# A depthwise convolution's taps on TensorE: from full diagonals, one tap at a time, to stacked diagonals in four column tiles, four taps at a time

## The reference, cut to what matters

```python
def conv_mixer(h, w_pw1, b_pw1, w_dw, b_dw, cg, cb, w_out, b_out):
    a, gt = jnp.split(h @ w_pw1 + b_pw1, 2, axis=-1)
    y = a * jax.nn.sigmoid(gt)
    y = lax.conv_general_dilated(y, w_dw[:, None, :], window_strides=(1,), padding='SAME',
                                 dimension_numbers=('NWC', 'WIO', 'NWC'),
                                 feature_group_count=D_MODEL) + b_dw
    y = jax.nn.silu(layer_norm(y, cg, cb))
    return y @ w_out + b_out
```

## Time and profile before

| What | us |
|---|---|
| Time before, median of 3 runs | 3671.02 |
| Lowest and highest of them | 3669.53, 3674.19 |
| Span of the profiled execution | 3670.5 |
| TensorE busy in it | 3537.7 (96%) |
| VectorE busy | 2182.4 (59%) |
| ScalarE busy | 1522.9 (41%) |
| GpSimd busy | 389.3 (11%) |

### The profile page before, as it was taken

One profiled execution on the slowest core, in us unless ns is written; L12 is line 12 of the kernel. 1 busy time (PEld: TensorE's weight loads), 2 busy tenths in 40 slices (PEclk: granted clock), 3 DMA queues, 4 the chain that ended last, 5 costly groups with the idle time before them and its releaser, 6 DMA issues. The chain is left out here.

```text
span 3670.5 us, 45735 instructions
## 1 busy us (share of the span) xinstructions
PE 3537.7 (96%) x18060; PEld 2922.5 (80%) x18060; DVE 2182.4 (59%) x2931; ACT 1522.9 (41%) x1713; POOL 389.3 (11%) x315
## 2 busy tenths in 40 slices
PE   8999999999999999999998999999998998999998
PEld 6888888756888888888758888877887777888886
DVE  7545446538654467556897433553226236999998
ACT  4111111537422233222446222453545235778776
POOL 2000000200120011000111100100000002333331
PEclk9999999999999999999999999999999998999999
DMA  6323323210244335444202322231221325999997
GB/s 258 125 81 104 115 89 102 66 58 1 70 149 138 111 119 171 144 156 160 72 21 70 103 92 98 81 117 55 86 69 62 117 101 204 365 366 360 366 374 297
DMA packets 315246, 522.43 MB, mean 142 GB/s; under 512 B 18517, under 2 KB 274562, under 8 KB 289217
## 3 DMA queue, kind: packets, MB, share of 16 engines
q1 hardware_dynamic: 304032, 507.06, 39.8%
q0 software_dynamic: 11040, 12.91, 1.0%
HBM read 519.91 MB, written 25.17 MB: 149 GB/s over the span
## 5 line engine op out<-in xcount | busy, mean ns | idle before, releaser
L541 PE MATMUL banks<-operand_hi,trunk_weights_hi 128*128 128x512 f32 (+1 forms) x1568 | 566.9, 362 | 21.5 <-DVE operand_lo L939 5.7
L541 PE MATMUL banks<-operand_lo,trunk_weights_hi 128*128 128x512 f32 (+1 forms) x1568 | 556.8, 355 | 0.0
L541 PE MATMUL banks<-operand_hi,trunk_weights_lo 128*128 128x512 f32 (+1 forms) x1568 | 556.7, 355 | 0.0
L541 PEld LDWEIGHTS banks<-operand_hi,trunk_weights_hi 128*128 128x128 f32 x1568 | 297.2, 190 | 69.3 <-issue 14.4
L541 PEld LDWEIGHTS banks<-operand_hi,trunk_weights_lo 128*128 128x128 f32 x1568 | 297.2, 190 | 41.9
L541 PEld LDWEIGHTS banks<-operand_lo,trunk_weights_hi 128*128 128x128 f32 x1568 | 297.4, 190 | 41.4 <-issue 0.5
L4311 DVE TENSOR_TENSOR ex_w_lo<-weight_ring,ex_w_hi 128x2048 fp32r<-128x2048 f32 x128 | 291.7, 2293 | 41.7 <-ACT ex_w_hi L4239 41.7
L1335 DVE TENSOR_TENSOR trunk_weights_lo<-weight_ring,trunk_weights_hi 128x2048 fp32r<-128x2048 f32 x90 | 206.1, 2290 | 176.9 <-ACT trunk_weights_hi L1290 176.9
L4239 ACT ACTIVATE ex_w_hi<-weight_ring 128x2048 fp32r<-128x2048 f32 x128 | 245.2, 1917 | 76.9 <-PE banks L4137 63.9
L1290 ACT ACTIVATE trunk_weights_hi<-weight_ring 128x2048 fp32r<-128x2048 f32 x90 | 171.7, 1908 | 216.5 <-PE banks L541 216.4
L541 PE MATMUL banks<-trunk_hidden_hi,trunk_weights_hi 128*128 128x512 f32 (+1 forms) x672 | 233.2, 347 | 3.4 <-DVE trunk_hidden_lo L1353 1.4
(11 more groups left out here) (612 smaller groups left out, 7451.6 us busy)
## 6 DMA issues: line engine op xcount, KB each, us to landing
weight_ring<-ffn_w SPq DMA_DIRECT2D x120, 1024.0 KB, 5.2
weight_ring<-w_mod SPq DMA_DIRECT2D x72, 1024.0 KB, 5.1
weight_ring<-w_gate SPq DMA_DIRECT2D x64, 1024.0 KB, 6.8
weight_ring<-w_up SPq DMA_DIRECT2D x64, 1024.0 KB
room<-w_down SPq DMA_DIRECT2D x64, 1024.0 KB, 7.2
weight_ring<-w_in SPq DMA_DIRECT2D x26, 1024.0 KB, 5.2
weight_ring<-ffn_w SPq DMA_DIRECT2D x16, 768.0 KB, 4.3
weight_ring<-o_w_pw SPq DMA_DIRECT2D x8, 1024.0 KB, 5.3
```

The lines of the kernel that those rows point to most:

```text
L541: ins = pe.matmul(bank[:, at:at + width], w, x[:, at:at + width], start=start and n == 0, stop=stop and n == len(passes) - 1)
```

## The change

TensorE's share of the taps is now done in fours. For a block b of 32 channels of a tile, four copies of Y's 32 rows, shifted by 0, 1, 2 and 3 tokens, are stacked on the 128 partitions. One product with a 128x32 stationary operand, four 32x32 diagonals one under the other, then does four taps of 32 channels. Four such products, one a block, write to PSUM partitions 0, 32, 64 and 96 and so use four column tiles of TensorE. A group g is these four products; it does taps 4g to 4g+3 of a tile.

- `GROUPS_ON_PE` is 4 for tiles 0 to 5 (16 taps, before 10 or 11) and 7 for tiles 6 and 7 (28 taps, before 12). VectorE has 15 taps left a tile, and 3 for the last two.
- The stacked copies are made by DMAs that ScalarE issues, 16 a tile (`act_shifts`), into three sets of buffers. They lie in unused room: the spare, the third region of the split weights, and `acc`.
- GpSimd makes the stacked diagonals from a folded identity, 16 or 28 small instructions a tile (`pool_taps`), from columns that VectorE has spread over the partitions in 16 copies (`dve_columns`). The diagonals lie in the second half of `k.X`.
- TensorE waits once a tile for the diagonals and the copies, and signals once.
- At the end, ScalarE's first weight split of the next stage waits for tile 5's taps, and VectorE adds tiles 4 and 5 after its own taps of the last pair.

```diff
         if m >= 4:
             pe.wait_ge(self.s_out, m - 3)
-        for w in range(ON_PE[m]):
-            n = self.first_diag[m] + w
-            pe.wait_ge(self.s_diag, n + 1)
-            pe.matmul(self.bank(m), self.diag[:, n % 8, :], self.Y[:, m, w:w + S], start=w == 0, stop=w == ON_PE[m] - 1).then_inc(self.s_tap, 1)
-
-    def act_diagonals(self, act, upto):
-        for n in range(self.n_diag, upto):
-            m = max(j for j in range(KD) if self.first_diag[j] <= n)
-            if n >= 8:
-                act.wait_ge(self.s_tap, n - 7)
-            act.activation(self.diag[:, n % 8, :], self.k.ident[:], ACT.Copy, scale=self.wdw((n - self.first_diag[m]) * KD + m)).then_inc(self.s_diag, 1)
-        self.n_diag = upto
+        pe.wait_ge(self.s_diag, m + 1)
+        pe.wait_ge(self.s_shift[m % 3], (m // 3 + 1) * 16 * STACK * STACK)
+        for g in range(GROUPS_ON_PE[m]):
+            for b in range(STACK):
+                ins = pe.matmul(self.bank(m)[b * BLOCK:(b + 1) * BLOCK], self.tap(m, b, g), self.shifted[m % 3][b][:, STACK * g:STACK * g + S],
+                                start=g == 0, stop=g == GROUPS_ON_PE[m] - 1)
+        ins.then_inc(self.s_tap, 1)
+
+    def tap(self, m, b, g):
+        n = b * MAX_GROUPS + g
+        return self.taps[:, 4 * (m % 2) + n // 8, BLOCK * (n % 8):BLOCK * (n % 8) + BLOCK]
+
+    def act_shifts(self, act, m):
+        if m == 0:
+            act.wait_ge(self.s_edges, 2)
+        act.wait_ge(self.s_value, m + 1)
+        if m >= 3:
+            act.wait_ge(self.s_tap, m - 2)
+        width = S + STACK * (GROUPS_ON_PE[m] - 1)
+        for b in range(STACK):
+            for j in range(STACK):
+                act.dma_start(self.shifted[m % 3][b][j * BLOCK:(j + 1) * BLOCK, 0:width],
+                              self.Y[b * BLOCK:(b + 1) * BLOCK, m, j:j + width]).then_inc(self.s_shift[m % 3], 16)
+
+    def dve_columns(self, dve):
+        first = COLUMN["o_w_dw"]
+        of_taps = self.k.col[:, first:first + STACK * MAX_GROUPS * KD].rearrange("p (g j m) -> p j m g", j=STACK, m=KD)
+        for b in range(STACK):
+            for j in range(STACK):
+                dve.tensor_copy(self.columns[j * BLOCK:(j + 1) * BLOCK, :, b, :], of_taps[b * BLOCK:(b + 1) * BLOCK, j, :, :]).then_inc(self.s_spread, 1)
+
+    def pool_taps(self, pool, m):
+        if m == 0:
+            pool.wait_ge(self.s_spread, STACK * STACK)
+        if m >= 2:
+            pool.wait_ge(self.s_tap, m - 1)
+        for b in range(STACK):
+            for g in range(GROUPS_ON_PE[m]):
+                ins = pool.tensor_scalar(self.tap(m, b, g), self.k.fold[:], self.columns[:, m, b, g:g + 1], 0.0, ALU.mult, ALU.add)
+        ins.then_inc(self.s_diag, 1)
...
         self.act_hi(act, 0, 3, 0)
+        for m in (0, 1):
+            self.act_shifts(act, m)
         for q in range(1, 4):
             if q < 3:
                 self.act_hi(act, 0, 2 * q + 2, 0)
             self.act_gates(act, 2 * q)
-            self.act_diagonals(act, min(upto(2 * q - 2) + 8, upto(2 * q)))
             if q < 3:
                 self.act_hi(act, 0, 2 * q + 3, 0)
-            self.act_diagonals(act, upto(2 * q))
+            for m in (2 * q, 2 * q + 1):
+                self.act_shifts(act, m)
...
-        for step in range(TAPS - min(ON_PE[m] for m in pair)):
+        for step in range(TAPS - STACK * GROUPS_ON_PE[2 * q]):
...
-ON_PE = (10, 10, 11, 11, 11, 11, 12, 12)
+STACK = P // BLOCK
+GROUPS_ON_PE = (4, 4, 4, 4, 4, 4, 7, 7)
+MAX_GROUPS = 7
+SHIFTED = S + STACK * (MAX_GROUPS - 1)
...
             for kk in range(KD):
                 n10.pool_rescale(pool, kk)
+                if kk == 3:
+                    conv.pool_taps(pool, 0)
+                    conv.pool_taps(pool, 1)
+            for m in range(2, KD):
+                conv.pool_taps(pool, m)
...
             conv.act_rest(act, lambda kk: n10.act_keep(act, kk))
+            act.wait_ge(conv.s_tap, 6)
             back.act_chunk(act, 0)
```

More of the change, by code:

```diff
@@ L360, in load_and_modulate @@
             sem("vectors_copied"), sem("silu"), sem("cond_hi"), sem("cond_lo"))
-        s_hi, s_lo, s_done, s_xt, s_xa, s_xd, s_row, s_gate, s_cols, s_ch, s_pad = (
+        s_hi, s_lo, s_done, s_xt, s_xa, s_xd, s_row, s_gate, s_cols, s_ch, s_pad, s_fold = (
             sem("w_hi"), sem("w_lo"), sem("products"), sem("x_turned"), sem("x_copied_act"), sem("x_copied_dve"), sem("mod_rows"),
-            sem("gate_rows"), sem("mod_columns"), sem("chain"), sem("cond_padded"))
+            sem("gate_rows"), sem("mod_columns"), sem("chain"), sem("cond_padded"), sem("fold"))
         block = st.enter_context(nc.Block())
@@ L402, in _ @@
             k.n_vec = n
+            pool.wait_ge(s_con, 16)
+            for i in range(0, P, BLOCK):
+                pool.tensor_copy(k.fold[i:i + BLOCK, :], k.ident[i:i + BLOCK, i:i + BLOCK]).then_inc(s_fold, 1)
         @block.tensor
@@ L1506, with __init__ @@
 class Convolution(Opening):
-    def __init__(self, k, st, name, bufs, base, Y, out, tmp, diag):
-        self.k, self.base, self.Y, self.out, self.tmp, self.diag = k, base, Y, out, tmp, diag
+    def __init__(self, k, st, name, bufs, base, Y, out, tmp, shifted, taps, columns):
+        self.k, self.base, self.Y, self.out, self.tmp = k, base, Y, out, tmp
+        self.shifted, self.taps, self.columns = shifted, taps, columns
         self.h_hi, self.h_lo, self.w_hi, self.w_lo = bufs
@@ L1516, in __init__ @@
             sem("weights_hi"), sem("weights_lo"), sem("tiles"), sem("gates"), sem("values"), sem("edges"))
-        self.s_diag, self.s_tap, self.s_acc, self.s_out = sem("diagonals"), sem("taps"), sem("sums"), sem("convolved")
+        self.s_spread, self.s_diag, self.s_tap, self.s_acc, self.s_out = (
+            sem("tap_columns"), sem("diagonals"), sem("taps"), sem("sums"), sem("convolved"))
+        self.s_shift = [sem(f"shifted{i}") for i in range(3)]
         self.loads = 8
@@ L1520, in __init__ @@
         self.n_acc = 0
-        self.first_diag = [sum(ON_PE[:m]) for m in range(KD + 1)]
-        self.n_diag = 0
     def sync(self, sp):
@@ L1624, in dve_taps @@
         last = {}
-        for step in range(TAPS - min(ON_PE[m] for m in pair)):
+        for step in range(TAPS - STACK * GROUPS_ON_PE[2 * q]):
             for m in pair:
-                w = ON_PE[m] + step
-                if w >= TAPS:
-                    continue
+                w = STACK * GROUPS_ON_PE[m] + step
                 x, out = self.Y[:, m, w:w + S], self.out[:, m, 0:S]
@@ L1657, in dve_rest @@
             self.dve_taps(dve, q, during)
+            if q == 3:
+                self.dve_out(dve, (4, 5))
             if q < 2:
@@ L1686, in region @@
         if c == 3:
-            return self.spare[part][:]
+            return self.spare[part]
         at = SLOT * (2, 0, 1)[c]
@@ L2040, in trunk @@
             conv_out = convolved.enter_context(nc.sbuf_tensor("trunk_convolved", [P, KD, S], F32))
-            spare = [convolved.enter_context(nc.sbuf_tensor(f"trunk_spare{i}", [P, SLOT], F32R)) for i in range(2)]
+            both = convolved.enter_context(nc.sbuf_tensor("trunk_spare", [P, 2 * SLOT], F32R))
+            spare = [both[:, SLOT * i:SLOT * i + SLOT] for i in range(2)]
+        pieces = lambda x, n, at=0: [x[:, at + SHIFTED * i:at + SHIFTED * i + SHIFTED].bitcast(F32) for i in range(n)]
+        in_spare, in_hi, in_lo = pieces(both, 7), pieces(w_hi, 3, 2 * SLOT), pieces(w_lo, 1, 2 * SLOT)
+        acc_row = acc[:].rearrange("p a b -> p (a b)")
+        n_columns = KD * STACK * MAX_GROUPS
+        shifted = [in_spare[0:4], in_spare[4:7] + [acc_row[:, n_columns:n_columns + SHIFTED]], in_hi + in_lo]
+        columns = acc_row[:, 0:n_columns].rearrange("p (m b g) -> p m b g", m=KD, b=STACK)
         bufs = (h_hi, h_lo, f_hi, f_lo, w_hi, w_lo, tmp, acc)
@@ L2047, in trunk @@
         conv = base(Convolution(k, st, "c_in", in_bufs, at[-1], room[:].rearrange("p (k t) -> p k t", k=KD), conv_out, tmp,
-                                acc[:].rearrange("p a (b c) -> p (a b) c", c=P)))
+                                shifted, k.X[:, :, S:S + HALF], columns))
         back = base(Halves(k, st, "c_out", in_bufs, spare, at[-1]))
```

8 lines of the change are left out of this document (5 added, 3 removed).

## The result

The changed kernel takes 3677.09 us (median of 20 runs, 3668.77 to 3685.65), the one before 3669.78 us beside it (20 runs). The ratio is 1.0019, with a 95% interval of 1.0013 to 1.0026: 7 us slower, by less than the 0.2% named in the prediction. The forecast was 3655, and 3671 the end of its range.

The account below looks back on a forecast made before the run. TensorE and VectorE were taken as balanced bounds of the stage. The walk's 24 us gain less 3 for the clock and 5 for GpSimd slowing VectorE gave 16 us less, so 3655 us; range 3640 to 3671 (0.82).

Parts of the forecast that it names:

- TensorE's part: TensorE's taps: 38 groups of four overlapping products at 0.87 us a group, 32.8 us in place of 76.0.
- Rivals 1 and 2: TensorE's taps: 1, half overlap, 1.73 us a group, 3664, chance 0.13; 2, no overlap, 3727 or 3757, chance 0.09.
- VectorE's part: VectorE's taps: loses 64 of 160, 42.6 us; gains 16 copies at 0.16 us, 2.4 us.
- ScalarE's part: ScalarE's queue: 88 diagonals go (32.8 us), 128 DMA issues come at 0.41 us each, 52 us in all.
- the prediction's walk: The stage stepped through pair by pair, each step at its later input: end at 1896.5 us, 24.2 us less.
- the clock: TensorE idles some 12 us ahead of tile 6, whose groups then run at a lower clock: 3 us on the path.
- GpSimd's part: GpSimd's 152 diagonals at 0.2 us, 30 us in all; its work slows VectorE, 5 us left after waits.
- The chain: VectorE and ScalarE wait for each other in turns: VectorE 3.6 us at chunk 4, 11 at chunk 6.
- Rival 3: Queues eat the gain: ScalarE's issue 0.55 us or more, or GpSimd's diagonal 0.4 or more; about 3668 us, chance 0.08.

Follow-up runs that it names:

- e3: The changed kernel with only the order of a tile's products changed, all groups of one block before the next block; 3693.97 us (one run).
- e7: As e1, but each DMA split in two of half the columns, 256 issues with the same bytes; 3713.47 us (one run).
- e1: The changed kernel with the 128 shift DMAs issued by SyncE instead of ScalarE; 3661.84 us, ratio 0.9979 to before.
- e4: The changed kernel with all 28 diagonals for tiles 0 and 1 but one for each later tile; 3682.49 us, ratio 1.0033 to before.
- e8: The changed kernel with GpSimd making one diagonal a tile, used by all its products; 3675.25 us, ratio 1.0012 to before.
- e10: The changed kernel with ScalarE issuing 10 of a tile's 16 DMAs, SyncE 6, and one GpSimd diagonal a tile; 3656.89 us, stage 20.5 us shorter than before.
- e5: As e1, but ScalarE issues the DMAs of blocks 0 and 1 of each tile, SyncE those of 2 and 3; 3662.34 us, ratio 0.9977 to before.
- e6: As e1, but ScalarE makes the 152 diagonals and GpSimd none; 3652.19 us, ratio 0.9946 to before.

## Why the prediction was wrong

- **TensorE's part** was right: tiles overlap, 0.86 us a group (I took 0.87), loads included. Rivals 1 and 2 did not occur. That the four tiles overlap by being four column tiles is shown by e3.
- **VectorE's part** was right but for the copies: 0.23 us each (3.69 us in all), where I took 0.16.
- **ScalarE's part is the step that failed.** "I choose 0.41 and keep 0.33 to 0.50"; it is 0.64 from one copy to the next and 0.67 with the pauses. I priced copies inside the core by SyncE's loads from outside, 0.47 us apart, and even took something off; but these copies cost more than that from the second one on, on ScalarE and on SyncE alike. What in a copy costs it was not found: not its bytes (e7), and not a full queue. With 0.67 for 0.41, and nothing else changed, the prediction's walk ends 4.6 us behind before instead of 24.2 ahead. With its 3 us for the clock that is 7.6 us, where the stage measures 7.2. e1 shows that the price lies on ScalarE: moved to SyncE the same issues cost 15 us less.
- **GpSimd's part** was mis-sized too: "0.2 us is an estimate, between 0.1 and 0.35". It is 0.27 alone and 1.03 beside VectorE's taps. I also charged it to the wrong engine: VectorE was to lose 0.38 us per busy us of GpSimd, while beside the diagonals it is GpSimd that waits and VectorE that keeps its pace (e1). What does hold VectorE are GpSimd's operations on whole tiles: the rescaled tiles in the change, e4, e8 and e10, the sums in e5. In the change all this is mostly hidden, since VectorE's waits for ScalarE let GpSimd through: 2.7 us by the stages of e8 and the change, where I had put 5. With the issues gone it costs 10.5 us (e6 against e1), though e6 moves the diagonals rather than dropping them. The two terms hide each other, and mending one alone gives half.
- **The chain** was right, as e10's stage and its two waits show at nearly the prices that I had taken. At the measured price of an issue the walk agrees too, with 7.6 against 7.2 us. Some luck is in both agreements: smaller errors, such as the copies and GpSimd's rescaled tiles beside VectorE, nearly cancel. The walk is not what to distrust; its inputs are.
- **The clock.** The window of 0.58 between tiles 5 and 6 fits the forecast. Tile 6's groups took 7.9 us where seven at 0.86 take 6.0, but this is not on the path, since tile 7 then waits 3.3 us for its copies. Tile 7's took 9.1 us, at a granted clock of 0.68, between the landing of its last copies and the last addition: 3.1 us on the path, the 3 us that I had put there for tile 6.
- **Rival 3** is what happened, by its first condition; the norm did not have to wait for GpSimd's sums. It had 0.08 and 3668 us, both too low: its walk reached only to 3675. The earlier trace rows shows two loads from outside; nothing in the trace before bounded the price of a copy inside the core from above, and the range should have said so by reaching over 3680.

## What to carry to other kernels

Price a series of DMAs by a series of the same kind: loads from outside stood 0.47 us apart, copies of 32 rows inside the core 0.64, whatever the length of a row, and two queues side by side each kept that pace. All this time the engine that issues does nothing else, though the profile counts it as idle. Such a series belongs on an engine that nobody waits for. Before small instructions go to GpSimd, ask what VectorE does meanwhile: between VectorE's two-input operations they took four times as long. Before large ones go there, ask the same for VectorE's sake. Where two mis-sized terms hide each other, mend both before judging the idea.
